# A two-direction state-space scan in one kernel: the forward and backward in-chunk matrices are added before one product with x, and GpSimd cuts off the wrong side of the diagonal

## The chip, the cores and the metric

The kernel runs on one core of a Trainium2 chip. The metric is the device time of one launch in microseconds, the median of several runs. It is a single program in which five engines (TensorE, VectorE, ScalarE, GpSimd and SyncE, in the profile PE, DVE, ACT, POOL and SP) run lists of instructions of their own and meet at semaphores.

## The reference, cut to what matters

Two blocks of a model over 512 tokens of width 1024 are computed. The first holds attention beside a state-space mixer that runs in both directions of time, and then an MLP; the second holds a gated recurrence and an attention with compressed keys. Only the mixer's scan is touched here.

```python
def segsum(a):                       # a: steps dt * A, per head
    cs = jnp.cumsum(a, axis=-1)
    diff = cs[..., :, None] - cs[..., None, :]
    return jnp.where(jnp.tril(...), diff, -jnp.inf)

def ssd_chunked(xdt, a, bm, cm):     # chunks of 128 tokens, 4 of them
    CB = jnp.einsum("bclgn,bcsgn->bgcls", Cc, Bc)
    M = CB[:, :, None] * jnp.exp(segsum(A))
    y_diag = jnp.einsum("bgrcls,bcsgrp->bclgrp", M, X)
    ...                              # states carried from chunk to chunk
    y_off = jnp.einsum("bclgn,cbgrpn,bgrcl->bclgrp", Cc, prev, jnp.exp(A_cs))
    return (y_diag + y_off).reshape(b, s, h, p)

y_fwd = ssd_chunked(xf * dt_f[..., None], dt_f * A[0], bm, cm)
y_bwd = flip(ssd_chunked(flip(xf * dt_b[..., None]), flip(dt_b * A[1]), flip(bm), flip(cm)))
y = y_fwd + y_bwd + ssd_D[:, None] * xf
```

There are 32 heads of width 64, 4 groups of 8 heads that share B and C, and a state of 128.

## The kernel before, in words

**Weights.** All weight matrices come as one stream of slabs of 128 x 512 (`SLAB`, 4 blocks of 128 x 128). SyncE loads slab s into one of 4 buffers `w_raw`, once GpSimd has finished slab s - 4. ScalarE rounds it to `w_hi` (L602, in `hi_upto`), GpSimd subtracts to get the rest `w_lo` (L560, in `low`), each into one of 7 buffers. TensorE waits for `lo_done` at the first block that it takes from a slab (`weights`, L1051) and does three products for each block of 128 rows (L1056, L1057, L1058). A tile of 8 blocks takes two slabs, one `so` tile (4 blocks) one slab.

**The scan.** The heads go by in 16 pairs i = 0 to 15 (`PAIRS`), 4 pairs for each group g. `between(i)` names the weight tiles that TensorE computes in pair i: the projection `xs` of the next pair, in some pairs the next group's `B` or `C`, from the second group on two output tiles `so` of the group before, and `z` of the next pair (in the last pair `ga` tiles). Their order and so the slab numbers are fixed at build time. With s0 for the first slab of `between(i)[0]`, slab s0 + 4 is the first slab of the `z` tile in pairs 2 to 5, 8, 9 and 12 to 14, of an `so` tile in pairs 6, 7, 10 and 11, and of `ga` in pairs 0 and 15; in pair 1 it belongs to the next pair's `xs`. So in pairs 2 to 15 TensorE needs it after four slabs of the same pair.

**One pair on each engine.** TensorE (L1178 to L1235) turns x (L1185) into bank `XT`, in a group's first pair also B (L1194) and the product CB (L1198); then the first tile of `between(i)`, the chunk states (L1211, L1212), the other tiles, and at the end the y product: 28 matmuls with 64 columns of weights and 128 columns of data, for each chunk X_f with M_f (L1226), the two state terms (L1229, L1232) and X_b with M_b (L1234). VectorE scales x four times out of PSUM (L1729), multiplies the decayed C (L1741), does the convolution of the next `xs` (L1648, L1655), carries the states (L1759), multiplies M by CB (L1771, two instructions of 128 x 1024, one for each direction, CB masked by a triangle at L1737), and after the y product forms the gated y (L1785, L1787). ScalarE takes the gated y (`b_hi`, L719; its square, L614), then Exp of 2048 cumulated sums (L692), up to two `w_hi`, and the exponents of M:

```python
a(A(Dm[:, r, w], csB[:, r, w], ACT.Abs, bias=csT[:, c, h:h + 1]))
```

sixteen of 128 x 128 in a pair (L701), with one Exp of 128 x 1024 after each eight (L704, scale -1). GpSimd's list is fixed too: `low(n)` slab by slab, and at the slab numbers in `stops` something else ahead of `low`: at s0 + 4 of pair i the addition of the square of pair i - 1 (`add_square`, L514). ScalarE's `hi_upto` runs 6 slabs ahead of the tile that is named (`AHEAD`).

Of the kernel before, what the change touches and what calls it, by code (L numbers as in the profile page):

```python
# [13 lines left out]
P = 128  # L14
# [250 lines left out]
def build(nc, d):  # L265

    with ExitStack() as ctx:
# [50 lines left out]
        with Arena():  # L318
# [4 lines left out]
            with Arena():  # L323
# [3 lines left out]
                XS = [sb(n, [P, NCH, P]) for n in ("X_state_f", "X_state_b", "X_f", "X_b")]  # L327
# [3 lines left out]
                CB = [sb(n, [P, SEQ]) for n in ("CB_f", "CB_b")]  # L331
# [5 lines left out]
                dtx = sb("dt_work2", [P, NCH, R2])  # L337
                dtF = Dm[0:R2, 1, :]
# [73 lines left out]
        wdec, decb = sem("decay_state"), sem("decay_chunk")  # L412
        csb_in, e_ready, ed_ready = sem("cs_in"), sem("C_decay"), sem("M_exp")
# [79 lines left out]
        def _(pool):  # L493
# [58 lines left out]

            turns = {}
# [10 lines left out]
            stops = sorted({0, fill_at, *turns, *squares, *heads, N_SLABS} - {n for n in (*turns, *squares) if n > N_SLABS})  # L564
            for s, end in zip(stops, stops[1:]):
                for name in turns.get(s, ()):
                    rotate(name)
                for norm, k in squares.get(s, ()):
                    add_square(norm, k)
# [20 lines left out]
        def _(act):  # L590
# [73 lines left out]
            hi_upto(slab_of(("C", 0)) + AHEAD)  # L664
            act.wait_ge(cs_done, 1)
# [18 lines left out]
            for i in range(PAIRS):  # L684
# [8 lines left out]
                if between(i):  # L693
                    hi_upto(slab_of(between(i)[0]) + AHEAD)
                for r in range(4):
                    h = (r // 2) * N_SSD + 2 * i + r % 2
                    for c in range(NCH):
                        w = slice(c * P, (c + 1) * P)


                        a(A(Dm[:, r, w], csB[:, r, w], ACT.Abs, bias=csT[:, c, h:h + 1]))  # L701
                    if r % 2:
                        a.settle()
                        A(Dm[:, r - 1:r + 1, :], Dm[:, r - 1:r + 1, :], ACT.Exp, scale=-1.0).then_inc(ed_ready, 1)  # L704
# [330 lines left out]
        def _(pe):  # L1035
# [142 lines left out]
            for i in range(PAIRS):  # L1178
# [3 lines left out]
                if i:  # L1182
                    pe.wait_ge(xs_sc, i)
                for c in range(NCH):
# [22 lines left out]
                pe.wait_ge(cb_ev, 2 * (g + 1))  # L1207
# [9 lines left out]
                pe.wait_ge(m_ready, 2 * (i + 1))  # L1217
                pe.wait_ge(ce_ready, i + 1)
# [4 lines left out]
                for c in range(NCH):  # L1223
# [3 lines left out]
                    if c:  # L1227
                        for hh, hp in enumerate(halves):
                            mm(YP[hp, w], prev[:, 0, c - 1, hp], Ex[:, hh, w], start=False, stop=False)  # L1229
                    if c < NCH - 1:  # L1230
                        for hh, hp in enumerate(halves):
                            mm(YP[hp, w], prev[:, 1, c, hp], Ex[:, 2 + hh, w], start=False, stop=False)  # L1232
                    for hh, hp in enumerate(halves):
                        ins = mm(YP[hp, w], XS[3][:, c, hp], Dm[:, 2 + hh, w], start=False, stop=True)  # L1234
# [1146 lines left out]
```

## Time and profile before

| | |
|---|---|
| median of 3 runs | 1685.29 us (1682.51 to 1687.72) |
| the profiled execution's own time | 1687.85 us |
| its span in the trace | 1685.9 us |
| TensorE, granted clock over the span | 0.984 of full |
| the scan's 16 pairs in the trace | about 88 to 470 us |

A timeline row gives start and duration in us, the engine, the line, the operation, output<-inputs and a count; a bracket holds the idle time of the engine before it and what ended it. Two records of a 128 x 128 fp32 matmul or activation belong to one instruction in some groups ("x4" in the y product are two matmuls). Durations of instructions on one engine overlap at their ends, so prices are taken from start to start where they follow each other.

### The profile page before, as it was taken

How to read it: one execution, taken by the hardware profiler on the slowest of the kernel's cores; microseconds unless marked ns; L12 is line 12 of the kernel's file. 1: busy time of each engine (PE TensorE's matmuls, PEld its weight loads, DVE VectorE, ACT ScalarE, POOL GpSimd, SP SyncE). 2: the span in 40 equal slices, each digit the busy share in tenths (PEclk: the TensorE clock that was granted, in tenths of full speed). 3: DMA queues.
4: the chain of work that ended last, by engine and by line, in shares of the span. 5: the costliest groups of instructions: out<-in, count | busy, mean ns of one | idle time of the engine just before them, and what ended most of it. 6: DMA issues, size and time to landing. Idle time of an engine off the chain costs nothing.

```text
span 1685.9 us, 23864 instructions
## 1 busy us (share of the span) xinstructions
PE 1610.3 (96%) x8328; PEld 1332.5 (79%) x8328; DVE 1029.6 (61%) x1355; ACT 745.6 (44%) x1357; POOL 779.7 (46%) x546
## 2 busy tenths in 40 slices
PE   4899999999999999999999999999999979899997
PEld 4678888888878688888878888888887768777776
DVE  4788999889829788488352221212288845557562
ACT  2366556646624444322343232323477535423322
POOL 1245555656645610156644444444554446333424
PEclk9999999999999999999989999999999989999999
DMA  7233343444332200167523333333332233211102
GB/s 298 78 128 98 118 138 102 119 132 115 107 92 70 75 1 26 63 236 254 184 63 102 99 100 89 100 99 93 95 95 81 82 91 106 72 44 51 63 20 87
DMA packets 76245, 171.30 MB, mean 102 GB/s; under 512 B 8240, under 2 KB 8624, under 8 KB 72816
## 3 DMA queue, kind: packets, MB, share of 16 engines
q1 hardware_dynamic: 68832, 133.09, 25.9%
q10 hardware_dynamic: 7312, 36.83, 6.3%
q8 instruction: 67, 1.10, 0.3%
q14 instruction: 34, 0.28, 0.1%
HBM read 167.67 MB, written 2.23 MB: 101 GB/s over the span
## 4 chain that ended last, share of the span: by engine, by line
PE 72%; DVE 11%; issue 9%; POOL 4%; ACT 2%; DMA 1%; SPq 0%; ACTq 0%; DVEq 0%; POOLq 0%
PE bank L1056 19%; PE bank L1058 18%; PE bank L1057 18%; POOL w_lo L560 4%; PE bank L1291 3%; DVE ada_acc L1570 2%; DVE rstd L1807 2%; PE bank L1102 1%; PE bank L1489 1%; PE bank L1226 1%; DMA x_stream<-x 1%; PE bank L1282 1%; PE bank L1234 1%; PE bank L1140 1%; PE bank L1283 1%
## 5 line engine op out<-in xcount | busy, mean ns | idle before, releaser
L560 POOL TENSOR_TENSOR w_lo<-w_raw,w_hi 128x512 fp32r<-128x512 f32 x457 | 687.9, 1527 | 655.2 <-ACT w_hi L602 654.4
L1056 PE MATMUL bank<-a_hi,w_hi 128*128 128x512 f32 x1040 | 417.6, 402 | 10.3 <-DVE a_lo L1594 6.2
L1058 PE MATMUL bank<-a_hi,w_lo 128*128 128x512 f32 x1040 | 408.5, 393 | 0.0
L1057 PE MATMUL bank<-a_lo,w_hi 128*128 128x512 f32 x1040 | 407.9, 392 | 0.0
L602 ACT ACTIVATE w_hi<-w_raw 128x512 fp32r<-128x512 f32 x457 | 262.5, 620 | 162.8 <-PE bank L1058 133.0
L1056 PE MATMUL bank<-b_hi,w_hi 128*128 128x512 f32 x600 | 237.6, 396 | 9.8 <-POOL w_lo L560 9.5
L1056 PEld LDWEIGHTS bank<-a_hi,w_hi 128*128 128x128 f32 x1040 | 197.3, 190 | 58.4 <-issue 10.3
L1058 PE MATMUL bank<-b_hi,w_lo 128*128 128x512 f32 x600 | 235.6, 393 | 0.0
L1057 PE MATMUL bank<-b_lo,w_hi 128*128 128x512 f32 x600 | 235.2, 392 | 0.0
L1058 PEld LDWEIGHTS bank<-a_hi,w_lo 128*128 128x128 f32 x1040 | 197.0, 189 | 42.6
L1057 PEld LDWEIGHTS bank<-a_lo,w_hi 128*128 128x128 f32 x1040 | 197.7, 190 | 41.5 <-issue 1.9
L1056 PEld LDWEIGHTS bank<-b_hi,w_hi 128*128 128x128 f32 x600 | 114.0, 190 | 34.5 <-POOL w_lo L560 9.9
L1058 PEld LDWEIGHTS bank<-b_hi,w_lo 128*128 128x128 f32 x600 | 113.6, 189 | 24.4
L1057 PEld LDWEIGHTS bank<-b_lo,w_hi 128*128 128x128 f32 x600 | 114.0, 190 | 23.5
L1978 DVE SCALAR_TENSOR_TENSOR x_stream<-bank,small,x_stream 128x512 f32<-128x512 f32 x32 | 24.0, 750 | 140.4 <-PE bank L1058 140.4
L1971 DVE TENSOR_TENSOR tmp<-tmp 128x512 f32<-128x512 f32 x32 | 23.5, 735 | 119.7 <-ACT tmp L835 119.7
L701 ACT ACTIVATE M<-cs_rows,cs 128x128 f32<-128x128 f32 x256 | 78.0, 388 | 0.0
L1655 DVE SCALAR_TENSOR_TENSOR tmp<-bank,small,tmp 128x510 f32<-128x510 f32 (+1 forms) x96 | 72.0, 749 | 3.4
L514 POOL TENSOR_TENSOR square_sum<-square_sum,sq 128x512 f32<-128x512 f32 x31 | 41.0, 1324 | 64.6 <-ACT sq L614 64.6
L1570 DVE SCALAR_TENSOR_TENSOR ada_acc<-ada_piece,small,ada_acc 128x2048 f32<-128x2048 f32 x21 | 62.2, 2964 | 7.6 <-DMA ada_piece<-ada 6.2
L835 ACT ACTIVATE tmp<-bank 128x512 f32<-128x512 f32 x32 | 19.1, 598 | 99.1 <-PE bank L1058 99.1
L1291 PEld LDWEIGHTS bank<-v_and_ones,probs 128*128 128x128 f32 x512 | 60.2, 192 | 1.9 <-ACT gates_early L647 1.2
(327 smaller groups left out, 2473.7 us busy)
## 6 DMA issues: line engine op xcount, KB each, us to landing
w_raw<-ws SPq DMA_DIRECT2D x457, 256.0 KB, 2.7
cs_rows<-cs_scratch ACTq DMA_DIRECT2D x16, 1024.0 KB, 5.4
ada_piece<-ada ACTq DMA_DIRECT2D x16, 1024.0 KB, 4.9
ada_piece<-ada SPq DMA_DIRECT2D x8, 1024.0 KB, 15.0
x_stream<-x SPq DMA_DIRECT2D x1, 2048.0 KB, 16.5
x_stream<-x ACTq DMA_DIRECT2D x1, 2048.0 KB, 8.4
out<-x_stream SPq DMA_DIRECT2D x8, 256.0 KB, 2.1
rope_table<-rope ACTq DMA_DIRECT2D x1, 512.0 KB, 3.4
```

What stands on the lines that cost most here:

```text
L514: nc.gpsimd.tensor_tensor(sq_sum[:, :], first[:, :], sq[n % 2][:, :], ALU.add).then_inc(sq_added, 1)
L560: nc.gpsimd.tensor_tensor(wlo[b][:, :], raw[n % RAW_RING][:, :], r32(whi[b][:, :]), ALU.subtract)\
L602: A(whi[n % RING][:, :], raw[n % RAW_RING][:, :], ACT.Copy).then_inc(hi_done, 1)
L701: a(A(Dm[:, r, w], csB[:, r, w], ACT.Abs, bias=csT[:, c, h:h + 1]))
L1056: mm(out, lh, rh, start=first, stop=False)
L1057: mm(out, lh, rl, start=False, stop=False)
L1058: return mm(out, ll, rh, start=False, stop=last)
L1291: ins = mm(OQ[h % 2][:, i * W:(i + 1) * W], PT[:, c, i * P:(i + 1) * P], vv[:, c, h // 4, :], start=(c == 0 and i == 0), stop=(c == NCH - ...
L1570: V.scalar_tensor_tensor(into[:, :], src[:, :], csl[:, k:k + 1], into[:, :], ALU.mult, ALU.add).then_inc(ada_acc, 1)
L1655: ins = V.scalar_tensor_tensor(out[:, o], src[:, s], cwh[:, j * 24 + i:j * 24 + i + 1], out[:, o], ALU.mult, ALU.add)
L1807: V.reciprocal(rstd[:, :], std[:, :]).then_inc(qk_inv, 1)
L1978: inc_evac(V.scalar_tensor_tensor(xF[:, m, :], gb(name)[:, :], modc[:, 5 * KT + m:5 * KT + m + 1], xF[:, m, :], ALU.mult, ALU.add), name)
```

## The change

In-chunk matrices of both directions are added and multiplied with x once. The step dt goes into the exponent as its logarithm (`lnCs` = ln dt - cs), so x goes into the product unscaled. Since one side of the diagonal then has exponents that mean nothing, GpSimd writes -1e30 there (`mask_exponents`) between ScalarE's sixteen additions and its two Exp; its call stands in GpSimd's list at slab s0 + 4 of pair i, ahead of that stop's `add_square`.

```diff
--- before.py
+++ after.py
@@ -324,17 +324,18 @@
                 csB = sb("cs_rows", [P, 4, SEQ])
                 Ex = sb("C_decayed", [P, 4, SEQ])
                 Dm = sb("M", [P, 4, SEQ])
-                XS = [sb(n, [P, NCH, P]) for n in ("X_state_f", "X_state_b", "X_f", "X_b")]
+                XS = [sb(n, [P, NCH, P]) for n in ("X_state_f", "X_state_b", "X_tok")]
                 BF = [sb(f"B_feat{b}", [P, SEQ]) for b in range(2)]
                 CF = [sb(f"C_feat{b}", [P, SEQ]) for b in range(2)]
                 BT = sb("B_tok", [P, NCH, P])
-                CB = [sb(n, [P, SEQ]) for n in ("CB_f", "CB_b")]
+                CB = sb("CB", [P, SEQ])
                 prev = sb("states", [P, 2, 3, P])
                 xsF = [sb(f"x_feat{b}", [P, SEQ]) for b in range(2)]
                 R2 = 2 * N_SSD
                 dtT, csT, aT, wS, decB, dtw = (sb(n, [P, NCH, R2]) for n in ("dt", "cs", "a", "dt_decay", "chunk_decay",
                                                                               "dt_work"))
                 dtx = sb("dt_work2", [P, NCH, R2])
+                lnT, lnCs = dtx, sb("log_dt_minus_cs", [P, NCH, R2])
                 dtF = Dm[0:R2, 1, :]
                 csF = Dm[0:R2, 0, :]
             with Arena():
@@ -410,6 +411,8 @@
         a_ready, cs_done, cs_ev, tot_e, cs_sb, cs_dram = (sem(n) for n in ("dt_a", "cs_psum", "cs_tok", "decay_arg",
                                                                            "cs_rows_sb", "cs_rows_dram"))
         wdec, decb = sem("decay_state"), sem("decay_chunk")
+        dt_floor, ln_ready, lncs_ready, raw_exp, exp_masked, x_kept = (sem(n) for n in (
+            "dt_floor", "log_dt", "log_dt_minus_cs", "exponents", "exponents_masked", "x_by_token"))
         csb_in, e_ready, ed_ready = sem("cs_in"), sem("C_decay"), sem("M_exp")
         conv_th, conv_done, z_th = sem("conv_tanh"), sem("conv_done"), sem("z_tanh")
         xt_done, xs_sc, bt_done, bt_ev, cb_done, cb_ev = (sem(n) for n in ("x_turned", "x_scaled", "B_turned", "B_tok",
@@ -550,6 +553,19 @@
                 nc.gpsimd.tensor_tensor(t[3][:, :], t[j % 2][:, :], rope1[:, 0, :], ALU.mult).then_inc(rot_step, 1)
                 nc.gpsimd.tensor_tensor(t[2][:, :], t[2][:, :], rope1[:, 1, :], ALU.mult).then_inc(rot_step, 1)
 
+            def mask_exponents(i):
+
+
+                for dd in range(2):
+                    half, sign = Dm[:, 2 * dd:2 * dd + 2, :].rearrange("p r (c l) -> p (r c) l", c=NCH), 1 - 2 * dd
+                    pool.wait_ge(raw_exp, 2 * i + dd + 1)
+                    nc.gpsimd.affine_select(half, half, pattern=[[0, 2 * NCH], [sign, P]], compare_op=ALU.is_ge, fill=-1e30,
+                                            base=0, channel_multiplier=-sign).then_inc(exp_masked, 1)
+
+            masked_at = {}
+            for i in range(PAIRS):
+                masked_at.setdefault(slab_of((between(i))[0]) + 4, []).append(i)
+
             turns = {}
             for name in QK:
                 turns.setdefault(slab_of(name) + RING + (QK_AT[name] <= KVT), []).append(name)
@@ -561,10 +577,12 @@
                     .then_inc(lo_done, 1)
 
             fill_at = slab_of(("so", N_GROUPS - 1, KT - 1))
-            stops = sorted({0, fill_at, *turns, *squares, *heads, N_SLABS} - {n for n in (*turns, *squares) if n > N_SLABS})
+            stops = sorted({0, fill_at, *turns, *squares, *heads, *masked_at, N_SLABS} - {n for n in (*turns, *squares) if n > N_SLABS})
             for s, end in zip(stops, stops[1:]):
                 for name in turns.get(s, ()):
                     rotate(name)
+                for i in masked_at.get(s, ()):
+                    mask_exponents(i)
                 for norm, k in squares.get(s, ()):
                     add_square(norm, k)
                 for h in heads.get(s, ()):
@@ -662,6 +680,8 @@
             A(lt[:, RT:2 * RT], lt[:, 0:RT], ACT.Exp).then_inc(lam_l, 1)
             conv_act(("B", 0))
             hi_upto(slab_of(("C", 0)) + AHEAD)
+            act.wait_ge(dt_floor, 1)
+            A(lnT[:, :, :], lnT[:, :, :], ACT.Ln).then_inc(ln_ready, 1)
             act.wait_ge(cs_done, 1)
             A(csF, YP[0:R2, :], ACT.Copy).then_inc(cs_sb, 1)
             A(decB[:, :, :], STF[:, 0:NCH * R2], ACT.Exp).then_inc(decb, 1)
@@ -692,16 +712,20 @@
                 A(Ex[:, :, :], csB[:, :, :], ACT.Exp).then_inc(e_ready, 1)
                 if between(i):
                     hi_upto(slab_of(between(i)[0]) + AHEAD)
+                if i == 0:
+                    act.wait_ge(lncs_ready, 1)
                 for r in range(4):
                     h = (r // 2) * N_SSD + 2 * i + r % 2
                     for c in range(NCH):
                         w = slice(c * P, (c + 1) * P)
-
-
-                        a(A(Dm[:, r, w], csB[:, r, w], ACT.Abs, bias=csT[:, c, h:h + 1]))
+                        ins = A(Dm[:, r, w], csB[:, r, w], ACT.Identity, bias=lnCs[:, c, h:h + 1])
                     if r % 2:
-                        a.settle()
-                        A(Dm[:, r - 1:r + 1, :], Dm[:, r - 1:r + 1, :], ACT.Exp, scale=-1.0).then_inc(ed_ready, 1)
+                        ins.then_inc(raw_exp, 1)
+                act.wait_ge(xs_sc, i + 1)
+                A(XS[2][:, :, :], XT[:, :], ACT.Copy).then_inc(x_kept, 1)
+                for dd in range(2):
+                    act.wait_ge(exp_masked, 2 * i + dd + 1)
+                    A(Dm[:, 2 * dd:2 * dd + 2, :], Dm[:, 2 * dd:2 * dd + 2, :], ACT.Exp).then_inc(ed_ready, 1)
                 if i + 1 < PAIRS:
                     act.wait_ge(e_ready, i + 1)
                     act.wait_ge(ed_ready, 2 * (i + 1))
@@ -1181,6 +1205,7 @@
                 pe.wait_ge(conv_done, CONV_AT[("xs", i)] + 1)
                 if i:
                     pe.wait_ge(xs_sc, i)
+                    pe.wait_ge(x_kept, i)
                 for c in range(NCH):
                     ins = nc.tensor.transpose(XT[:, c * P:(c + 1) * P], xsF[i % 2][:, c * P:(c + 1) * P], ident)
                 ins.then_inc(xt_done, 1)
@@ -1204,7 +1229,7 @@
 
                 pe.wait_ge(xs_sc, i + 1)
                 pe.wait_ge(bt_ev, g + 1)
-                pe.wait_ge(cb_ev, 2 * (g + 1))
+                pe.wait_ge(cb_ev, g + 1)
                 if i:
                     pe.wait_ge(rec_done, i)
                 for c in range(NCH - 1):
@@ -1215,6 +1240,7 @@
                     mixer_tile(name)
 
                 pe.wait_ge(m_ready, 2 * (i + 1))
+                pe.wait_ge(x_kept, i + 1)
                 pe.wait_ge(ce_ready, i + 1)
                 pe.wait_ge(rec_done, i + 1)
                 if i:
@@ -1226,12 +1252,10 @@
                         mm(YP[hp, w], XS[2][:, c, hp], Dm[:, hh, w], start=True, stop=False)
                     if c:
                         for hh, hp in enumerate(halves):
-                            mm(YP[hp, w], prev[:, 0, c - 1, hp], Ex[:, hh, w], start=False, stop=False)
+                            ins = mm(YP[hp, w], prev[:, 0, c - 1, hp], Ex[:, hh, w], start=False, stop=(c == NCH - 1))
                     if c < NCH - 1:
                         for hh, hp in enumerate(halves):
-                            mm(YP[hp, w], prev[:, 1, c, hp], Ex[:, 2 + hh, w], start=False, stop=False)
-                    for hh, hp in enumerate(halves):
-                        ins = mm(YP[hp, w], XS[3][:, c, hp], Dm[:, 2 + hh, w], start=False, stop=True)
+                            ins = mm(YP[hp, w], prev[:, 1, c, hp], Ex[:, 2 + hh, w], start=False, stop=True)
                 ins.then_inc(y_done, 1)
             pe.wait_ge(nfull, KT)
             for m in range(KT):
@@ -1683,6 +1707,7 @@
             log1p(dtw[:, :, :], decB[:, :, :], dtx[:, :, :], wS[:, :, :])
             v(V.scalar_tensor_tensor(dtT[:, :, :], dtT[:, :, :], 0.0, wS[:, :, :], ALU.max, ALU.add))
             v.settle()
+            V.tensor_scalar(lnT[:, :, :], dtT[:, :, :], 1e-37, None, ALU.max).then_inc(dt_floor, 1)
             ve.wait_ge(sp_e, 2)
             V.scalar_tensor_tensor(aT[:, :, :], dtT[:, :, :], -1.0, tbc[:, None, R2:2 * R2].broadcast_to([P, NCH, R2]),
                                    ALU.mult, ALU.mult).then_inc(a_ready, 1)
@@ -1693,6 +1718,8 @@
             ve.wait_ge(cs_done, 1)
             v(V.tensor_scalar(csT[:, :, :], STB[:, 0:NCH * R2], -1.0, None, ALU.mult))
             v.settle()
+            ve.wait_ge(ln_ready, 1)
+            V.tensor_tensor(lnCs[:, :, :], csT[:, :, :], lnT[:, :, :], ALU.add).then_inc(lncs_ready, 1)
             ve.wait_ge(decb, 1)
             V.tensor_tensor(dtw[:, :, :], STF[:, 0:NCH * R2].rearrange("p (c r) -> p c r", c=NCH), csT[:, :, :],
                             ALU.add).then_inc(tot_e, 1)
@@ -1724,7 +1751,7 @@
                 if i:
                     ve.wait_ge(y_done, i)
                 xt = XT[:, :].rearrange("p (c h d) -> p c h d", c=NCH, h=2)
-                for n, (buf, tab, dd) in enumerate(((XS[0], wS, 0), (XS[1], wS, 1), (XS[2], dtT, 0), (XS[3], dtT, 1))):
+                for n, (buf, tab, dd) in enumerate(((XS[0], wS, 0), (XS[1], wS, 1))):
                     h0 = dd * N_SSD + 2 * i
                     ins = V.tensor_tensor(buf[:, :, :].rearrange("p c (h d) -> p c h d", h=2), xt,
                                           tab[:, :, h0:h0 + 2, None].broadcast_to([P, NCH, 2, HD]), ALU.mult)
@@ -1733,10 +1760,7 @@
                     gated_low(i - 1)
                 if pg == 0:
                     ve.wait_ge(cb_done, g + 1)
-                    for buf, tri in zip(CB, (trif, trib)):
-                        V.tensor_tensor(buf[:, :].rearrange("p (c l) -> p c l", c=NCH),
-                                        STF[:, :].rearrange("p (c l) -> p c l", c=NCH),
-                                        tri[:, None, :].broadcast_to([P, NCH, P]), ALU.mult).then_inc(cb_ev, 1)
+                    V.tensor_copy(CB[:, :], STF[:, :]).then_inc(cb_ev, 1)
                 ve.wait_ge(e_ready, i + 1)
                 V.tensor_tensor(Ex[:, :, :], Ex[:, :, :], CF[g % 2][:, None, :].broadcast_to([P, 4, SEQ]), ALU.mult)\
                     .then_inc(ce_ready, 1)
@@ -1765,11 +1789,12 @@
                 for name in names:
                     if name[0] in ("B", "C"):
                         conv_taps(name)
-                ve.wait_ge(cb_ev, 2 * (g + 1))
-                for dd in range(2):
-                    ve.wait_ge(ed_ready, 2 * i + dd + 1)
-                    V.tensor_tensor(Dm[:, 2 * dd:2 * dd + 2, :], Dm[:, 2 * dd:2 * dd + 2, :],
-                                    CB[dd][:, None, :].broadcast_to([P, 2, SEQ]), ALU.mult).then_inc(m_ready, 1)
+                ve.wait_ge(cb_ev, g + 1)
+                ve.wait_ge(ed_ready, 2 * (i + 1))
+                V.tensor_tensor(Dm[:, 0:2, :], Dm[:, 0:2, :], Dm[:, 2:4, :], ALU.add).then_inc(m_ready, 1)
+                ve.wait_ge(m_ready, 2 * i + 1)
+                V.tensor_tensor(Dm[:, 0:2, :], Dm[:, 0:2, :], CB[:, None, :].broadcast_to([P, 2, SEQ]), ALU.mult)\
+                    .then_inc(m_ready, 1)
                 for name in names:
                     if name[0] == "so":
                         so_evac(name)
```

## Rows read from the trace of the kernel before

**Rows 1.** The page, busy time and share of each engine.

```profile
PE 1610.3 (96%) x8328; PEld 1332.5 (79%) x8328; DVE 1029.6 (61%) x1355; ACT 745.6 (44%) x1357; POOL 779.7 (46%) x546
```

**Rows 2.** Busy time by stage: us, PE, PEld, DVE, ACT, POOL, clock, DMA share, GB/s.

```profile
88.00:470.00 382.00, 377.02 (x2471) 319.01 (x2471) 334.34 (x494) 239.64 (x488) 217.65 (x121) 1.00 0.38 115
470.00:1686.00 1216.00, 1172.95 (x5596) 964.04 (x5595) 641.00 (x789) 478.43 (x825) 543.49 (x409) 0.98 0.29 91
```

**Rows 3.** Who waited for whom, 88 to 470 us: total, times, longest.

```profile
POOL w_lo L560 <- ACT w_hi L602: 96.8, 26, 7.4
...
PE bank L1226 <- DVE M L1771: 4.3, 2, 2.4
```

**Rows 4.** Timeline of PE in pair 9.

```profile
315.48 0.39 PE L1056 MATMUL bank<-a_hi,w_hi 128*128 128x512 f32 x1
...
321.01 0.44 PE L1226 MATMUL bank<-M,X_f 128*64 128x128 f32 x4
...
323.24 0.39 PE L1234 MATMUL bank<-M,X_b 128*64 128x128 f32 x4
323.46 0.39 PE L1226 MATMUL bank<-M,X_f 128*64 128x128 f32 x4
...
324.22 0.66 PE L1185 MATMUL bank<-consts,x_feat 128*128 128x128 f32 x4
```

**Rows 5.** Timeline of ACT in pair 9.

```profile
304.31 0.72 ACT L719 ACTIVATE b_hi<-x_feat,small 128x512 fp32r<-128x512 f32 x1 [4.13 <-DVE x_feat L1787]
...
305.46 1.91 ACT L692 ACTIVATE C_decayed<-cs_rows 128x2048 f32<-128x2048 f32 x1
...
308.31 2.44 ACT L701 ACTIVATE M<-cs_rows,cs 128x128 f32<-128x128 f32 x8
...
311.75 2.44 ACT L701 ACTIVATE M<-cs_rows,cs 128x128 f32<-128x128 f32 x8
314.21 1.06 ACT L704 ACTIVATE M<-M 128x1024 f32<-128x1024 f32 x1
```

**Rows 6.** Timeline of POOL in pair 9.

```profile
305.63 1.30 POOL L514 TENSOR_TENSOR square_sum<-square_sum,sq 128x512 f32<-128x512 f32 x1 [5.24 <-ACT sq L614]
306.89 6.32 POOL L560 TENSOR_TENSOR w_lo<-w_raw,w_hi 128x512 fp32r<-128x512 f32 x3
317.08 6.05 POOL L560 TENSOR_TENSOR w_lo<-w_raw,w_hi 128x512 fp32r<-128x512 f32 x3 [3.88 <-ACT w_hi L602]
```

**Rows 7.** Timeline of DVE in pair 9.

```profile
302.80 0.75 DVE L1785 SCALAR_TENSOR_TENSOR x_feat<-x_feat,params,bank 128x512 f32<-128x512 f32 x1 [1.90 <-PE bank L1234]
...
305.39 0.68 DVE L1729 TENSOR_TENSOR X_f<-bank,dt 128x512 f32<-128x512 f32 x1
...
316.74 1.22 DVE L1771 TENSOR_TENSOR M<-M,CB_f 128x1024 f32<-128x1024 f32 x1
317.88 2.32 DVE L1771 TENSOR_TENSOR M<-M,CB_b 128x1024 f32<-128x1024 f32 x1
```

**Rows 8.** Groups of POOL over the whole span: busy us, mean ns, idle before.

```profile
L499 POOL MEMSET k_hi<- 1x512 f32 x4 | 2.1, 519 | 0.2
```

**Rows 9.** The chain that ended last, a first pair of a group.

```profile
280.94 0.89 PE bank L1198 x8
```

**Rows 10.** Timeline of PE at two waits, and the clock after them by stage.

```profile
126.18 0.70 PE L1226 MATMUL bank<-M,X_f 128*64 128x128 f32 x4 [2.40 <-DVE M L1771]
...
178.16 0.44 PE L1226 MATMUL bank<-M,X_f 128*64 128x128 f32 x4 [1.93 <-DVE M L1771]
...
126.00:128.00 2.00, 1.82 (x18) 0.50 0.68 258
...
178.00:179.00 1.00, 0.84 (x16) 1.00 0.00 0
```

**Rows 11.** Timeline of ACT and DVE ahead of the scan.

```profile
59.00 1.28 ACT L659 ACT_TABLE_LOAD   x1
...
82.40 0.81 DVE L1648 TENSOR_SCALAR tmp<-bank,small 128x512 f32<-128x512 f32 x1 [0.97 <-PE bank L1058]
```

## The prediction

> **What bounds the kernel now.** The page comes first: TensorE is busy for 96% of the span [rows 1]. Read by stage, it is busy for 377 of the scan's 382 us, VectorE for 334, ScalarE for 240, GpSimd for 218 [rows 2]. So the scan is bound by TensorE, with VectorE close behind. The table of waits says where TensorE stands still: only twice, 4.3 us in all, for VectorE's M in front of the y product [rows 3]. GpSimd, on the other hand, waits 97 us for `w_hi` [rows 3]. That is idle time, but not time at any place: its list is in order.
>
> So I follow one ordinary pair, pair 9, on each engine, as distances from the end of the y product of pair 8, which frees VectorE at 302.80 [rows 7]:
> - ScalarE takes the gated y at 304.31, Exp of the C decay at 305.46, two `w_hi`, and the first eight exponents at 308.31; the last Exp ends at 315.27 [rows 5].
> - GpSimd adds the square at 305.63, then makes the `w_lo` of slabs s0 + 4 to s0 + 6 from 306.89 to 313.21, 2.1 us each; it then waits until 317.08 [rows 6].
> - TensorE starts on slab s0 + 4 (the `z` tile) at 315.48, on the y product at 321.01, on the next pair at 324.22 [rows 4]. The first of those three slabs is ready by about 309.0, 6.5 us early. This lead is what the change spends.
>
> **The change part by part.**
>
> *TensorE, removed.* Eight of 28 matmuls of the y product. Two of them take 0.22 us from start to start [rows 4], so eight take 0.87 us, over 16 pairs 13.9 us. This is the whole gain in reach while TensorE sets the pace.
>
> *VectorE.* Two of four scalings of x go, 0.60 to 0.68 us each [rows 7]; in a group's first pair two masked copies of CB become one. M still takes two instructions of 128 x 1024, an addition and a product, each between 1.22 and 2.32 us [rows 7], but the first now waits for both Exp. VectorE gets 1.3 us shorter in a pair. It is not the bound in pairs 4 to 15, so this is worth nothing there. M is not late next: after the second select come Exp 1.06 and at most 2 x 2.32 for M, 5.7 us, while TensorE behind the same select still needs the square, one `w_lo` and a `z` tile of 5.5 us (315.48 to 321.01), 8.9 us.
>
> *ScalarE.* Sixteen Identity for sixteen Abs, taken at the same price (bias and shape are the same), and no Exp between the two eights: they end at 308.31 + 2 x 2.44 = 313.2. Then a copy of x out of PSUM, about 0.6, and the two Exp, each behind its select. What queues behind a waiting Exp is the load of the next cumulated sums, the tanh, four `w_hi` and z's tanh. ScalarE idles 4.13 us at the end of a pair [rows 5], so these fit; I add nothing.
>
> *Ahead of the scan.* Ln needs its table, and Exp and Tanh theirs again: two loads of 1.28 us and one activation. A floor under dt and the sum `lnCs`, 128 x 256 each, add about 0.7 us to VectorE. VectorE waits 0.97 us for TensorE there [rows 11], which hides it; ScalarE has gaps too. I take 0, at worst 3 (both loads in the open). The Trainium skill (ScalarE: Activation LUTs, What ACT_TABLE_LOAD costs) puts a switch at about 2.66 us, as the load is followed by a drain of 1.38. The trace shows 1.28 for the load itself; by the page the worst case would be 6 instead of 3.
>
> *GpSimd, added.* 32 selects of 128 x 1024. The trace has none. The nearest rows: a memset of 512 elements on one partition takes 0.519 us, so 1.04 for 1024 with one stream (write) [rows 8]; an addition of 128 x 512 takes 1.30, so 2.6 for 1024 with three streams (two reads and a write) [rows 6]. Next to VectorE's SBUF work `w_lo` stretches from 1.3 to 2.1, which makes the upper end 4.2. A select reads one stream and writes one. I take 1.5 us, nearer the lower end. The Trainium skill (GPSIMD Engine Reference, section 4.1, Engine selection) says that operations with one input run at roughly VectorE's line rate. With VectorE's 1.22 us for 128 x 1024 [rows 7] that would be about 1.2 us; the sum below would come out at 30 instead of 35 us. No row here shows it.
>
> *Where it is put.* The selects of pair i stand in GpSimd's list ahead of the square and of `w_lo` of slab s0 + 4. The second select can't start before ScalarE's last Identity, at 313.2, where the `w_lo` of three slabs used to be finished. So:
>
> | step | start | length |
> |---|---|---|
> | second select | 313.25 | 1.5 |
> | square | 314.75 | 1.30 |
> | `w_lo` of s0 + 4, beside VectorE's M | 316.05 | 2.1 |
> | TensorE may start on it | 318.15 | |
>
> TensorE wants it at 315.48. It stands for 2.7 us, and the 0.87 saved comes off behind it: +1.8 us for an ordinary pair. All of it is counted from the end of the last y product, so it comes again in each pair in which s0 + 4 is needed within the pair, pairs 2 to 15. In a group's first pair (4, 8, 12) TensorE has some 1.3 us of transposes and CB ahead of the first tile [rows 9], ScalarE some 0.6 of B copy: stall 2.0, +1.1. In pair 3 there is already a wait of 1.93 [rows 10] that the new one takes the place of: 2.7 - 1.93 - 0.87 = -0.1. Pairs 0 and 1 don't need the slab: -0.9 in pair 0; in pair 1 M comes 0.6 later through ScalarE and the select, against the 0.87: -0.3. Sum: 10 x 1.8 + 3 x 1.1 - 0.1 - 1.2 = +20 us.
>
> *The clock.* After the wait of 2.40 us TensorE's granted clock was 0.50 (1.2 GHz), after the one of 1.93 it stayed 1.00 (2.4 GHz) [rows 10]; the low stretch took 3.4 us. At half speed that costs 1.7 us, directly ahead of the y product. Stalls of 2.7 lie above the one that cost, those of 2.0 near the one that didn't. I take 9 of 14: +15 us.
>
> Together +35 us: 1687.9 + 35 = 1723 for the profiled execution. The median of the runs shown lies 2.6 us below its own time, so the forecast for the median is 1720 us.
>
> **Bounds.** Select 1.04 and `w_lo` 1.3, both at their lower ends: the slab is ready at 316.9, stall 1.4, +0.5 for ten pairs, -0.2 for three, -1.4 and -1.2 for the rest, no fall of the clock: +2 us, 1688. Select 2.6: the first one ends at 313.4, the second at 316.0, the slab is ready at 319.4, stall 3.9: 10 x 3.05 + 3 x 2.35 + 1.1 - 1.2 = +37, and 13 falls of the clock +22: +60, 1745. Select 4.2: stall 7.1, +82 and 24: 1791.
>
> **The rivals.**
> - *The clock holds.* Stalls of 2.7 us between long busy stretches leave it at 1.00, as 1.93 did. Then only +20, 1705 us (with a select of 1.04 to 2: 1695 to 1712).
> - *The select is slow.* At 2.6 us or more it is worth +60 to +106: 1745 to 1791. For it speaks that every two-input operation of GpSimd costs 2.5 ns an element; against it that a select has one input.
> - *The select is quick and nothing contends.* +2 to +8, 1687 to 1693 us, the lower bound above.
> - *Faster: the lead is long enough.* TensorE never waits for `w_lo` and keeps the eight matmuls: -13.9, 1671 us. The place is slab s0 + 4; select and `w_lo` together must end within 315.48 - 313.25 - 1.30 = 0.9 us for all of it, and within 1.8 us to break even. The lower bounds sum to 2.3. It needs a select under 0.5 us, or exponents that are ready a microsecond earlier than the Abs were.
>
> **How the numbers follow.** No change is within 0.3%, 5 us: about what a measurement of this kernel can tell. Chances: the forecast, waits for `w_lo` and a clock that falls in most pairs, 0.53; the clock holds 0.18; slow select 0.13; quick select 0.09, of which 0.06 is no change; faster 0.07. So slower 0.87, same 0.06, faster 0.07. The range from 1688 to 1752 leaves out the faster case and most of the quick one below, and the slow select above its first third, together 2 in 10.
>
> **What the profile after would show.** Right: in the table of waits TensorE at L1056 waits for `w_lo` of GpSimd in 14 pairs, 2 to 3 us each, where it had none; in GpSimd's timeline two selects, then the square, then `w_lo`, the first select starting 8.0 us and the second 10.4 behind the end of a y product; granted clock 0.50 for 3.4 us after many of the waits; the y product 2.3 us instead of 3.2; from 470 us on everything as before, shifted. Wrong: a select far from 1.5 us moves the sum by 10 us for each 0.7 us or so, and past 2.4 us twice as fast, as the first then delays the second; a `w_lo` that is ready in time takes the whole forecast away; a wait of TensorE for M or for the copy of x would mean that I misread which of them comes last.

## The result, and the profile after

The changed kernel took 1702.89 us (median of 5 runs, 1699.44 to 1704.95), the kernel before 1685.29 us (5 runs, 1682.51 to 1687.72). The ratio is 1.0101, 95% interval 1.008 to 1.0121: slower by 17.6 us. The forecast was 1720 us, +35: the right direction, and twice the size. The profiled executions are 1699.44 us (span 1697.6) and 1687.85 us, 11.6 apart; the first is the fastest of its kernel's runs, the second lies above all five of its own.

The page and its groups first. The next fence is from the page of the changed kernel, busy time of each engine and two groups of GpSimd (out<-in, count, busy us, mean ns, idle before).

```profile
PE 1601.0 (94%) x8072; PEld 1318.9 (78%) x8072; DVE 1009.9 (59%) x1321; ACT 755.1 (44%) x1376; POOL 773.0 (46%) x578
...
L576 POOL TENSOR_TENSOR w_lo<-w_raw,w_hi 128x512 fp32r<-128x512 f32 x457 | 646.9, 1438 | 582.0 <-ACT w_hi L620 581.2
...
L562 POOL TENSOR_SCALAR_AFFINE_SELECT M<-M 128x1024 f32<-128x1024 f32 x32 | 34.9, 1092 | 164.4 <-ACT M L721 164.4
```

TensorE has 256 records less [rows 1], as it should with 128 matmuls gone, and yet the span is longer. A select of 128 x 1024 takes 1.09 us. GpSimd now stands in front of the selects for 164 us, with work behind them in its list.

The table of waits, 88 to 490 us, which answers to [rows 3]:

```profile
ACT w_hi L620 <- DMA w_raw<-ws: 100.0, 32, 6.1
...
DVE tmp L1698 <- ACT tmp L671: 36.0, 14, 3.8
...
PE bank L1080 <- POOL w_lo L576: 14.9, 10, 2.5
PE bank L1080 <- issue: 5.0, 4, 1.3
...
PE bank L1252 <- DVE M L1796: 4.8, 2, 4.5
```

TensorE waits 14 times at the first product of a slab (L1080, before L1056): ten times put down to `w_lo`, four times named issue, 1.26 us each, at the `so` tiles of pairs 6, 7, 10 and 11, where GpSimd's `w_lo` ends 0.1 us before. That is 19.9 us in the 14 pairs, where it had none. The two lines on top are new too, and I hadn't foreseen them: ScalarE waits for loaded slabs, and VectorE for the tanh of z.

A wait costs more than its idle time, as pair 2 shows:

```profile
145.16 0.39 PE L1082 MATMUL bank<-a_hi,w_lo 128*128 128x512 f32 x1
146.84 0.47 PE L1080 MATMUL bank<-a_hi,w_hi 128*128 128x512 f32 x1 [1.29 <-POOL w_lo L576]
147.15 0.39 PE L1081 MATMUL bank<-a_lo,w_hi 128*128 128x512 f32 x1
```

From start to start there are 1.68 and 0.31 us where otherwise 0.23 and 0.23 stand: 1.54 us for an idle time of 1.29, 0.25 more. By an estimate from this row, the 14 waits cost 19.9 + 14 x 0.25 = 23.4 us.

Pair 9 in the changed kernel. GpSimd, against [rows 6]:

```profile
304.98 4.49 POOL L576 TENSOR_TENSOR w_lo<-w_raw,w_hi 128x512 fp32r<-128x512 f32 x3
318.14 1.09 POOL L562 TENSOR_SCALAR_AFFINE_SELECT M<-M 128x1024 f32<-128x1024 f32 x1 [8.68 <-ACT M L721]
320.48 1.09 POOL L562 TENSOR_SCALAR_AFFINE_SELECT M<-M 128x1024 f32<-128x1024 f32 x1 [1.25 <-ACT M L721]
321.54 1.27 POOL L517 TENSOR_TENSOR square_sum<-square_sum,sq 128x512 f32<-128x512 f32 x1
322.77 9.99 POOL L576 TENSOR_TENSOR w_lo<-w_raw,w_hi 128x512 fp32r<-128x512 f32 x6
```

TensorE, against [rows 4]:

```profile
321.25 0.39 PE L1082 MATMUL bank<-b_hi,w_lo 128*128 128x512 f32 x1
324.17 0.75 PE L1080 MATMUL bank<-a_hi,w_hi 128*128 128x512 f32 x1 [2.54 <-POOL w_lo L576]
```

VectorE, against [rows 7]:

```profile
309.45 0.69 DVE L1698 SCALAR_TENSOR_TENSOR tmp<-tmp,bank 128x512 f32<-128x512 f32 x1 [3.79 <-ACT tmp L671]
310.06 0.74 DVE L1810 SCALAR_TENSOR_TENSOR x_feat<-x_feat,params,bank 128x512 f32<-128x512 f32 x1
...
322.89 2.22 DVE L1794 TENSOR_TENSOR M<-M 128x1024 f32<-128x1024 f32 x1
325.14 2.18 DVE L1796 TENSOR_TENSOR M<-M,CB 128x1024 f32<-128x1024 f32 x1
```

ScalarE, against [rows 5]:

```profile
306.25 0.63 ACT L620 ACTIVATE w_hi<-w_raw 128x512 fp32r<-128x512 f32 x1 [5.33 <-DMA w_raw<-ws]
...
308.84 0.58 ACT L671 ACTIVATE tmp<-bank 128x512 f32<-128x512 f32 x1
...
315.55 4.78 ACT L721 ACTIVATE M<-cs_rows,log_dt_minus_cs 128x128 f32<-128x128 f32 x16
```

Read as the prediction set it up: from the first step on the finished y product (VectorE at 310.06) to the second select 10.4 us, then select, square, `w_lo`, and TensorE goes on in the moment that this is ready. Two things differ from the working. `w_lo` is ready 1.4 us behind its start, not 2.1. The 2.1 was the mean of three durations that lie far apart; here they are one by one (before, pair 9), and behind them the first two `w_lo` of the last GpSimd row above:

```profile
306.89 1.75 POOL L560 TENSOR_TENSOR w_lo<-w_raw,w_hi 128x512 fp32r<-128x512 f32 x1
308.59 3.35 POOL L560 TENSOR_TENSOR w_lo<-w_raw,w_hi 128x512 fp32r<-128x512 f32 x1
311.91 1.29 POOL L560 TENSOR_TENSOR w_lo<-w_raw,w_hi 128x512 fp32r<-128x512 f32 x1
```

```profile
322.77 1.26 POOL L576 TENSOR_TENSOR w_lo<-w_raw,w_hi 128x512 fp32r<-128x512 f32 x1
323.99 2.25 POOL L576 TENSOR_TENSOR w_lo<-w_raw,w_hi 128x512 fp32r<-128x512 f32 x1
```

In these rows the one that starts second pays. `w_lo` starts 0.12 us ahead of VectorE's M and takes 1.26; M ends 1.08 us behind the end of that `w_lo` and so takes 2.22 instead of 1.22; the next `w_lo` starts during M and ends 1.13 us behind M's end, 2.25. The 3.35 us belong to a `w_lo` that started beside the decayed C (307.40 to 310.79).

And pair 8's y product was finished at about 308.7, but VectorE took it only at 310.06, since its list has z's gate ahead of it, which waited for a tanh, which stood behind a `w_hi`, which waited 5.33 us for the load of its slab, and that load waits for a `w_lo`. The lateness comes round once more.

The clock, by stage (the column behind POOL is the granted share):

```profile
120.00:140.00 20.00, 15.50 (x96) 13.34 (x95) 15.90 (x23) 11.20 (x22) 7.99 (x5) 0.83 0.33 106
215.00:235.00 20.00, 17.89 (x103) 14.34 (x102) 15.95 (x25) 10.83 (x20) 13.28 (x9) 0.91 0.42 132
320.00:335.00 15.00, 12.46 (x80) 9.94 (x79) 10.76 (x20) 6.20 (x11) 12.28 (x8) 0.89 0.57 169
445.00:460.00 15.00, 12.83 (x80) 10.14 (x79) 11.93 (x20) 7.11 (x14) 12.58 (x9) 0.89 0.54 161
```

The missing share of each row times its length comes to 8.5 us, against 1.7 before (one fall, [rows 10]). Not all of it costs time: in pair 1 the clock fell 1.6 us before TensorE went on (before, 0.4 us), so 0.8 and 0.2 us of the missing share lie in the wait itself. What is left is 7.7 against 1.5: +6.2, where I had put +15.

### The profile page after: what moved, and what is told of

Its sections match the earlier page's. It is cut to its first block, busy times and chain, and to the rows that moved or that the text cites. A ratio compares the mean times of both kernels' runs of the same rounds, so it can differ in the third digit from the quotient of the medians.

```text
span 1697.6 us, 23401 instructions
## 1 busy us (share of the span) xinstructions
PE 1601.0 (94%) x8072; PEld 1318.9 (78%) x8072; DVE 1009.9 (59%) x1321; ACT 755.1 (44%) x1376; POOL 773.0 (46%) x578
## 4 chain that ended last, share of the span: by engine, by line
PE 65%; issue 9%; DVE 9%; POOL 7%; ACT 7%; DMA 2%; SPq 0%; ACTq 0%; POOLq 0%; DVEq 0%
PE bank L1080 17%; PE bank L1082 17%; PE bank L1081 17%; POOL w_lo L576 6%; PE bank L1315 3%; ACT M L721 3%; DVE rstd L1832 2%; PE bank L1126 1%; POOL square_sum L517 1%; ACT C_decayed L712 1%; DMA w_raw<-ws 1%; PE bank L1513 1%; DMA x_stream<-x 1%; ACT w_hi L620 1%; PE bank L1306 1%
## 5 line engine op out<-in xcount | busy, mean ns | idle before, releaser
L576 POOL TENSOR_TENSOR w_lo<-w_raw,w_hi 128x512 fp32r<-128x512 f32 x457 | 646.9, 1438 | 582.0 <-ACT w_hi L620 581.2
L1080 PE MATMUL bank<-a_hi,w_hi 128*128 128x512 f32 x1040 | 419.7, 404 | 25.1 <-POOL w_lo L576 16.4
L620 ACT ACTIVATE w_hi<-w_raw 128x512 fp32r<-128x512 f32 x457 | 267.0, 621 | 261.5 <-PE bank L1082 129.8
L1080 PEld LDWEIGHTS bank<-a_hi,w_hi 128*128 128x128 f32 x1040 | 198.3, 191 | 76.7 <-issue 27.6
L1080 PE MATMUL bank<-b_hi,w_hi 128*128 128x512 f32 x600 | 236.7, 395 | 14.8 <-POOL w_lo L576 9.5
L1080 PEld LDWEIGHTS bank<-b_hi,w_hi 128*128 128x128 f32 x600 | 113.2, 189 | 40.8 <-POOL w_lo L576 9.9
L562 POOL TENSOR_SCALAR_AFFINE_SELECT M<-M 128x1024 f32<-128x1024 f32 x32 | 34.9, 1092 | 164.4 <-ACT M L721 164.4
L721 ACT ACTIVATE M<-cs_rows,log_dt_minus_cs 128x128 f32<-128x128 f32 x256 | 76.5, 388 | 0.0
L632 ACT ACTIVATE sq<-x_stream 128x512 f32<-128x512 f32 x40 | 24.9, 624 | 83.8 <-DVE x_stream L1967 32.8
```

Of the source, the lines that this page charges most:

```text
L562: nc.gpsimd.affine_select(half, half, pattern=[[0, 2 * NCH], [sign, P]], compare_op=ALU.is_ge, fill=-1e30, base=0, channel_multiplier=-sig ...
L576: nc.gpsimd.tensor_tensor(wlo[b][:, :], raw[n % RAW_RING][:, :], r32(whi[b][:, :]), ALU.subtract)\
L620: A(whi[n % RING][:, :], raw[n % RAW_RING][:, :], ACT.Copy).then_inc(hi_done, 1)
L632: A(sq[n % 2][:, :], src, ACT.Square, scale=scale).then_inc(sq_ready, 1)
L721: ins = A(Dm[:, r, w], csB[:, r, w], ACT.Identity, bias=lnCs[:, c, h:h + 1])
L1080: mm(out, lh, rh, start=first, stop=False)
```

## The experiments

Theory A is the prediction's: the loss is the place in GpSimd's list, where the `w_lo` of slab s0 + 4 queues behind the second select. Theory B: the loss is the longer way of M (ScalarE to GpSimd and back, then two dependent steps on VectorE), wherever the select stands. Theory C: the clock is most of it. All ratios are to the kernel before, measured on the same chip.

**The selects three slabs later.** Nothing else is changed.

```diff
-                masked_at.setdefault(slab_of((between(i))[0]) + 4, []).append(i)
+                masked_at.setdefault(slab_of((between(i))[0]) + 7, []).append(i)
```

> The selects stand three slabs later in GpSimd's list, ahead of w_lo of slab s0 + 7 instead of s0 + 4; everything else is the changed kernel. Theory A (the loss is the place: w_lo of s0 + 4 queued behind the second select): TensorE's waits at L1080 for w_lo in the scan, 20 us with those named issue, go to under 2 us, no fall of the clock in pairs 2 to 15, the eight matmuls saved show as 0.87 us less per pair, ratio to the kernel before 0.991 to 0.996. Theory B (the loss is the longer way of M over ScalarE, GpSimd and back, wherever the select stands): ratio 1.005 or more, waits of TensorE for M at the y product.

1673.44 us, ratio 0.9927 (0.9913 to 0.9942). The waits of its scan, 88 to 480 us:

```profile
ACT w_hi L620 <- DMA w_raw<-ws: 3.2, 5, 0.9
...
PE bank L1252 <- DVE M L1796: 4.5, 2, 2.5
PE bank L1080 <- ACT gates_early L665: 1.2, 1, 1.2
```

No wait for `w_lo` is left, and ScalarE's waits for loads went from 100 to 3 us. The way of M is as long as in the change, so theory B falls. One integer moved the kernel from 1% slower to 0.7% faster; this version beats both. Pair 1 is worth a look, GpSimd first, then M on VectorE, then the clock behind TensorE's wait for M:

```profile
120.01 2.27 POOL L562 TENSOR_SCALAR_AFFINE_SELECT M<-M 128x1024 f32<-128x1024 f32 x2
125.23 1.98 POOL L576 TENSOR_TENSOR w_lo<-w_raw,w_hi 128x512 fp32r<-128x512 f32 x1 [2.95 <-ACT w_hi L620]
```

```profile
123.60 1.22 DVE L1794 TENSOR_TENSOR M<-M 128x1024 f32<-128x1024 f32 x1
124.86 1.23 DVE L1796 TENSOR_TENSOR M<-M,CB 128x1024 f32<-128x1024 f32 x1
```

```profile
126.00:128.00 2.00, 1.86 (x34) 1.86 (x36) 2.00 (x3) 0.15 (x1) 1.22 (x1) 1.00 0.86 301
```

GpSimd runs nothing when either product of M starts, and they take 1.22 and 1.23; it is the `w_lo` that starts during the second that stretches, to 1.98. In the change a run of `w_lo` starts right behind the selects and M takes 2.25 and 2.17, 2.0 us of the 4.5 that TensorE waited in pair 1. And the clock stayed 1.00 behind a stall of 2.53 us.

**The square ahead of the selects.** Only the two calls at the same stop change places.

```diff
-                for i in masked_at.get(s, ()):
-                    mask_exponents(i)
                 for norm, k in squares.get(s, ()):
                     add_square(norm, k)
+                for i in masked_at.get(s, ()):
+                    mask_exponents(i)
```

> Only the order of two calls at the same stop is turned: the square of pair i - 1 ahead of the selects of pair i. Theory A: the square (1.3 us) leaves the chain behind the second select, each stall on s0 + 4 gets 1.3 us shorter or goes: 0 in the pairs that had 1.3 or less, about 1 in pairs 5, 9, 13, 14; with fewer falls of the clock the time drops by 15 to 20 us against the changed kernel, ratio to before 0.997 to 1.002. Theory B: as the changed kernel, 1.010.

1690.35 us, ratio 1.0032 (1.002 to 1.0044), just outside the expected range: 12 us less than the change, and slower than before still. TensorE's waits for `w_lo` fell from 14.9 (10 times) to 6.7 (5 times), those named issue from 5.0 to 3.3. The stalls of pairs 3, 4, 7, 8, 11 and 12 went, those of pairs 2 and 6 stayed at 1.25 and 1.11, and those of pairs 9 and 10 were 2.1, behind VectorE's two longest waits for the tanh (3.6 and 3.4 of 32.2 us). So the square's 1.3 us are in the chain, and something else feeds it.

**A select of almost nothing, in its place.** 8 instead of 1024 elements of each partition; the wrong side of the diagonal is not cut off, and the Exp have a scale of 0.001.

```diff
-                    nc.gpsimd.affine_select(half, half, pattern=[[0, 2 * NCH], [sign, P]], ...)
+                    part = half[:, 0:1, 0:8]
+                    nc.gpsimd.affine_select(part, part, pattern=[[0, 1], [sign, 8]], ...)
...
-                    A(Dm[:, 2 * dd:2 * dd + 2, :], Dm[:, 2 * dd:2 * dd + 2, :], ACT.Exp).then_inc(ed_ready, 1)
+                    A(Dm[:, 2 * dd:2 * dd + 2, :], Dm[:, 2 * dd:2 * dd + 2, :], ACT.Exp, scale=1e-3).then_inc(ed_ready, 1)
```

> The select covers 8 elements of each partition instead of 1024, with all its waits and in its place (the wrong side of the diagonal stays in M, and the Exp that follow have a scale of 0.001, so that their values stay finite). Theory A: a select of about 0.2 us takes 0.9 us out of each chain; stalls of 1.3 become 0.4, those of 2.1 to 2.5 about 1.3, ratio 0.998 to 1.003. Theory B with the select's own traffic as the cost: the same. Theory C (falls of the clock make most of the loss): granted clock 1.00 throughout pairs 2 to 15 takes 5 us more off.

1691.79 us, ratio 1.0043 (1.0029 to 1.0058), a little above what was expected. In its trace:

```profile
L563 POOL TENSOR_SCALAR_AFFINE_SELECT M<-M 128x8 f32<-128x8 f32 x32 | 6.2, 192 | 174.4 <-ACT M L722 174.4
```

The select shrank from 1.09 to 0.19 us, the stalls of pairs 2, 3, 6, 7 and 11 from 1.3 to about 0.4, those of pairs 5, 9, 13 and 14 only to 1.6 to 2.3, and those of pairs 8 and 10 grew, to 1.4 and 2.3. Even a select of nearly no length leaves the kernel slower than before: its length is worth 0.6 of the 1.7 points between the change and the selects at s0 + 7, its place all of them. The clock still fell in pairs 1 and 5, so what theory C expected of this run (1.00 in pairs 2 to 15) isn't met.

**Each select twice.**

```diff
+                    for turn in range(2):
+                        ins = nc.gpsimd.affine_select(half, half, ...)
+                        if turn == 0:
+                            ins.then_inc(mask_once, 1)
+                            pool.wait_ge(mask_once, 2 * i + dd + 1)
+                    ins.then_inc(exp_masked, 1)
```

> Each select is done twice, the second time on its own output. Theory A: the first select's double still fits ahead of the second half of the exponents (2.2 of 2.4 us), the second adds 1.1 us to each chain: stalls of 2.4 in pairs that had 1.3, 3.3 where there were 2.2; +12 to +15 us, and by the clock's falls (every stall above 2.4 us so far had one but one of 2.28 not) another 8 to 15: ratio 1.020 to 1.028. Theory B: less than +5 us.

1726.84 us, ratio 1.0251 (1.0234 to 1.0269), inside the expected range. TensorE's waits, 88 to 510 us:

```profile
PE bank L1087 <- POOL w_lo L583: 28.4, 10, 3.3
PE bank L1087 <- issue: 10.6, 4, 3.2
PE bank L1259 <- DVE M L1803: 5.7, 1, 5.7
```

39.0 us over 14 stalls instead of 19.9: 2.8 us each, close to the stall on which the prediction was made. With it the clock fell in the windows of 8 pairs of 15 (granted share 0.83 in pair 1, 0.89 to 0.91 over 15 to 20 us in seven more), and the time was 42.6 us above before: for such stalls the forecast loss of 35 us was about right (5.7 us of waiting for M in pair 1 are among the 42.6), but the stalls weren't such.

**The matmuls alone.** The kernel before, without the product of X_b and M_b (the backward in-chunk part is missing from y).

```diff
-                    for hh, hp in enumerate(halves):
-                        ins = mm(YP[hp, w], XS[3][:, c, hp], Dm[:, 2 + hh, w], start=False, stop=True)
```

> The kernel before, with the eight matmuls of X_b with M_b left out of each pair (so the backward in-chunk part is missing from y) and nothing else changed. The term of the prediction: 0.87 us for each pair, 13.9 us in all, ratio 0.9918 (0.990 to 0.993). If VectorE or ScalarE bound more of the scan than I read, less than 8 us, ratio above 0.995.

1672.55 us, ratio 0.9921 (0.9904 to 0.9937): -13.3 us by the ratio (12.6 between the medians) for the 13.9 worked out. The steady pairs took 20.67 and 26.1 us instead of 21.54 and 27.0. The gain in reach was rightly sized; the selects at s0 + 7 leave almost all of it.

**z's tanh ahead of the last `w_hi`.** The changed kernel, with ScalarE's last three `w_hi` of a pair behind the tanh instead of ahead of it.

```diff
-                tile_in(("z", i))
+                hi_upto(slab_of(("z", i)) + AHEAD - 3)
+                wait_tile(act, ("z", i))
...
                 A(zth[i % 2], gb(("z", i))[:, :], ACT.Tanh, scale=0.5).then_inc(z_th, 1)
+                hi_upto(slab_of(("z", i)) + AHEAD)
...
-                        hi_upto(slab_of(name) + AHEAD)
+                        hi_upto(slab_of(name) + AHEAD - 2)
```

> The changed kernel, with the w_hi of the last slabs of a pair moved behind z's tanh on ScalarE, so that the tanh doesn't wait for slabs whose load waits for the late w_lo. Theory A2 (a second loop makes the stalls of 2.1 to 2.5 out of 1.3: late w_lo, late load of w_raw, late w_hi, late tanh, late gated y, late exponents): the stalls of pairs 5, 9, 13, 14 go to 1.3 or less and VectorE's waits for the tanh, 36 us, to under 12; with three falls of the clock fewer 7 to 10 us less than the changed kernel, ratio 1.003 to 1.006. Rival: the load was hidden and these stalls come from the w_lo itself: as the changed kernel, 1.010.

1697.04 us, ratio 1.0066 (1.0049 to 1.0083): 6 us less than the change, but not because TensorE stands less. Its 14 stalls add up to 20.8 us (14.0 and 6.8 named issue) instead of 19.9. The second loop shows in their pattern: those of pairs 5, 9, 13 and 14 went from 2.1 to 2.5 down to 1.75, while those of pairs 6, 7, 10, 11 and 15 went up from 1.3 to about 1.7, and VectorE's wait for the tanh only halved. From its waits and VectorE's timeline:

```profile
DVE tmp L1700 <- ACT tmp L672: 18.9, 12, 2.3
PE bank L1082 <- POOL w_lo L576: 14.0, 10, 1.8
```

```profile
305.90 0.75 DVE L1812 SCALAR_TENSOR_TENSOR x_feat<-x_feat,params,bank 128x512 f32<-128x512 f32 x1 [1.03 <-PE bank L1257]
306.69 1.15 DVE L1814 TENSOR_TENSOR x_feat<-x_feat,tmp 128x512 f32<-128x512 f32 x1
```

The y product is now taken as soon as it is there, but the gating behind it takes 1.15 us instead of 0.69: the delayed `w_hi` bring `w_lo` to that place (GpSimd has two from 304.75 to 307.29), and a product with both inputs in SBUF stretches beside them. The 0.46 us fit the step from 1.3 to 1.75; no run takes them away by themselves.

What the 6 us are, the clock says. The change in the first fence, this run in the second, from pair 2 to pair 15:

```profile
140.00:480.00 340.00, 319.74 (x1877) 0.98 0.37 111
```

```profile
140.00:474.00 334.00, 312.91 (x1869) 1.00 0.36 113
```

This run has no fall there, the change has three, and in pair 1 it has one where the change has two behind each other: 3 x 1.7 us and about 1 more. With these falls gone and the stalls as large as before, the kernel is still 0.7% slower than the kernel before: theory C falls too.

**One and two slabs later.** As the first experiment, with + 5 and + 6 instead of + 7.

> The selects one slab later than in the change, at s0 + 5. Theory A: w_lo of s0 + 4 is made right behind the square, early; that of s0 + 5 is ready 2.4 us behind the start of the second select, some 13 us behind the end of the y product, while TensorE needs it at 15.5: no stall, the same time as with the selects at s0 + 7, ratio 0.991 to 0.995. Rival (the lead must be several slabs, since late w_lo delays the loads too): waits for w_lo remain, ratio above 0.997.

> The selects at s0 + 6, between the place that measured 0.998 (s0 + 5, where no wait for w_lo was left but late loads of w_raw still held ScalarE) and that at 0.993 (s0 + 7). If each w_lo that is made ahead of the selects also brings its load forward, ScalarE's waits for w_raw (100 us in the changed kernel, 46 at s0 + 5) fall below 30 and the ratio is 0.992 to 0.996. If the gap between the two is only chance of the clock, 0.996 to 0.999 again.

At s0 + 5: 1682.27 us, ratio 0.9984 (0.9972 to 0.9996). At s0 + 6: 1671.6 us, ratio 0.9939 (0.9925 to 0.9953). ScalarE's wait for loads, s0 + 5 in the first fence and s0 + 6 in the second:

```profile
ACT w_hi L620 <- DMA w_raw<-ws: 46.1, 29, 4.7
...
PE bank L1252 <- DVE M L1796: 6.5, 2, 4.5
```

```profile
ACT w_hi L620 <- DMA w_raw<-ws: 28.7, 13, 4.2
```

I was wrong on s0 + 5: no wait of TensorE for `w_lo` is left there, yet more than three quarters of the gain over the kernel before are missing (0.16 of 0.73 points are there). ScalarE's waits for loads fall 100, 46, 29, 3 us from + 4 to + 7, and the ratios 1.0101, 0.9984, 0.9939, 0.9927. At s0 + 5 TensorE waits for M 4.5 us in pair 1 as in the change, for a convolution in pair 10 (1.97 us) and for a gate in pair 15 (2.35 us). But the clock differs as well, s0 + 5 first, s0 + 7 second:

```profile
120.00:460.00 340.00, 328.50 (x1957) 0.98 0.37 117
```

```profile
120.00:450.00 330.00, 324.34 (x1964) 1.00 0.40 121
```

In the profiled execution of s0 + 5 it fell in pairs 1, 3 and 10, at s0 + 7 in none of them. That is about 5 of the 10.6 us by which the last y product starts later. So the late loads are at most half of the difference in these two executions, and that they cause the waits in pairs 10 and 15 is argued, not shown. Between + 6 and + 7 the intervals overlap.

**No Ln.** Copy with scale -1 in its place, so the exponents hold -dt instead of ln dt.

> The changed kernel with Copy (scale -1) in place of Ln, so no change of ScalarE's table ahead of the scan (the exponents then hold -dt in place of ln dt). By the prediction this part is hidden: less than 1 us. The trace of the changed kernel has the scan start 0.4 us later than before; by the Trainium skill's price of a switch it could be 5 us, ratio 1.007 instead of 1.010.

1702.99 us, ratio 1.0103 (1.008 to 1.0125): nothing measurable. ScalarE's two loads of a table cost 1.28 us each in the changed kernel's trace (76.21 and 78.42), and no run shows them in the time. The Trainium skill (ScalarE: Activation LUTs, What ACT_TABLE_LOAD costs) counts a drain of 1.38 us with each; the trace has 1.28 from the load's start to Ln's (77.50), and ScalarE was busy up to 76.19, so here nothing of a drain shows on either side.

## Why the prediction was wrong in size

**What held.** The place (slab s0 + 4, pairs 2 to 15), the order select, square, `w_lo`, the start of the first and second select 8.1 and 10.4 us behind VectorE's start on the finished y product (8.0 and 10.4 forecast), the 13.9 us of matmuls (13.3 measured), ScalarE's price for Identity, the hidden Ln, and that M is not what TensorE waits for from pair 4 on.

**What failed: the term for the stall.** "It stands for 2.7 us" was 1.26 to 1.31 us of idle time, 1.5 with what a wait costs on top, where nothing else was late. From the second select to TensorE's start there are 3.7 us in pair 9 (320.48 to 324.17), not 4.9. The select took 1.09 where I took 1.5, and `w_lo` 1.4 where I took 2.1. The Trainium skill (GPSIMD Engine Reference, section 4.1, Engine selection), roughly line rate for one input, was right: 1.09 against VectorE's 1.22. The memset row pointed to 1.04, and I moved away from it towards an operation with two inputs. For `w_lo` I carried over 2.1, the mean of 1.75, 3.35 and 1.29 beside the decayed C, to a place where it starts first and M pays. Both at their lower ends are what the prediction worked out under its bounds: a stall of 1.4 and +2 us in all. (One slip under the rivals: with the clock held, a select of 1.04 gives 14 x 0.46 = 6.4 us less than 1705, so 1699, not 1695.)

**The clock term** followed from the stall. I put 9 falls of 14 on stalls of 2.7 us; on stalls of 0.5 to 2.54 there were 3, and a doubled one in pair 1. With stalls of 2.8 (each select twice) there were 7 of 14. So the term was +6.2 instead of +15, and the one run with longer stalls speaks for the length of the stall as the reason.

**Two terms were missing**, and they hide how far off the first was. One stood in the prediction at nothing: "ScalarE idles 4.13 us at the end of a pair, so these fit; I add nothing." The idle time fitted, the order did not. The late `w_lo` delays the loads, these the `w_hi`, the tanh and the gated y, which starts the next pair's chain: the stalls of pairs 5, 9, 13 and 14 were 2.11, 2.54, 2.28 and 2.17 instead of 1.3, together 3.9 us. SyncE's longest wait for a `w_lo` before it may load was 17.0 us, against 9.7 in the kernel before and 8.6 with the selects at s0 + 7. And in pair 1 I took M at its old length, though the queued `w_lo` start exactly there: TensorE waited 4.5 us instead of about 3.0, 1.5 us more.

The account at the end of the scan, in the prediction's terms. It added up stalls of 10 x 2.7, 3 x 2.0 and 2.7 us, 35.7 in all; they cost 23.4, the 3.9 of the loop among them. So 20 - 12.3 (stalls) + 6.2 (clock) + 1.5 (M in pair 1) + 0.3 (a rest of M in pair 3) + 0.4 (scan starts later) = 16.1 us. Measured: the first product of x with M in pair 15 starts at 479.52 instead of 462.95, +16.6, less 0.87 for that block: 15.7.

Behind the scan the profiled execution gives 4 us back (11.7 between the spans) without any change in the code there. The clock of that part accounts for it: over all its falls its missing share is 26.8 us in the profiled execution of before and 22.2 in that of the change. One of them, before first, then the same stretch in the change:

```profile
1467.00:1477.00 10.00, 8.45 (x26) 0.66 0.41 111
```

```profile
1480.00:1490.00 10.00, 6.90 (x30) 1.00 0.52 131
```

So the profiled pair shows less than the medians, which are 17.6 apart.

## What to carry to other kernels

In an engine that works through a list in order, an inserted instruction costs above all the wait for its input, and its own length only on top: everything behind it starts after that. So look for what stands behind it and who needs that first, and put it behind the work that can be done early; here one integer made 1.7%. A wait taken away from the consumer isn't the end of it: the same work also frees buffers, and the loads behind them still come late when the direct wait is gone (46 us of ScalarE's waits at s0 + 5). And the mean of a group is no price: 2.1 us stood for 1.29 and for 3.35, and which of them applies depends on who starts first.

## What was unexpected of the hardware

- A GpSimd select of 128 x 1024 fp32 takes 1.09 us, of 128 x 8 0.19 us; an addition of 128 x 512 takes 1.27 to 1.30.
- Where a VectorE instruction with both inputs in SBUF meets `w_lo` on GpSimd, the one that starts second stretches, by about the rest of the first: M 2.22 us behind a `w_lo` of 1.26, the next `w_lo` 2.25 behind M, and `w_lo` 1.98 where M ran first at 1.23 (selects at s0 + 7).
- A stall of TensorE of 2.40 us was followed by a granted clock of 0.50 [rows 10], one of 2.53 us at the same place in another kernel by 1.00. Without the eight matmuls a stall of 2.41 us in pair 1 was followed by 1.00 (126 to 128 us) and one of 1.93 in pair 3 by 0.50 (176 to 178 us). The length alone doesn't decide.
